# Float32r halves for the output projection and the memory projections of block two, with weight slots that step around the gates

## The reference

```python
merged = (jax.nn.sigmoid(gate_a) * (y_a @ w_branch_a[l])
          + jax.nn.sigmoid(gate_b) * (y_b @ w_branch_b[l]))
x = x + merged @ w_out[l]
x = x + memory_attention(rms_norm_2(x, norm_mem[l]), rms_norm_2(mem, mem_tok_norm[l]), mem_wq[l],
                         mem_wkv[l], mem_q_norm[l], mem_k_norm[l], mem_wo[l])
...
def memory_attention(h, mem_n, wq, wkv, q_norm, k_norm, wo):
    q = rms_norm_2((h @ wq).reshape(bsz, seqlen, MEM_HEADS, MEM_HEAD_DIM_2), q_norm)
    k, v = split_cols(mem_n @ wkv, (MEM_DIM, MEM_DIM))
    k = rms_norm_2(k.reshape(bsz, n_mem, MEM_HEADS, MEM_HEAD_DIM_2), k_norm)
    ...
```

## Time and profile before

| | us |
|---|---|
| Median of three runs | 3002.8 |
| The three runs | 2996.65, 3004.51, 3002.8 |
| The profiled execution | 2996.5 |
| Its span in the trace | 2994.6 |
| TensorE busy | 2785.1 (93%) |
| VectorE busy | 1494.3 (50%) |
| ScalarE busy | 1028.2 (34%) |
| GpSimd busy | 129.5 (4%) |
| Mean granted clock of TensorE | 0.978 |

### The profile page before, as it was taken

One profiled execution on the slowest core, in us unless ns is written; L12 is line 12 of the kernel. 1 busy time (PEld: TensorE's weight loads), 2 busy tenths in 40 slices (PEclk: granted clock), 3 DMA queues, 4 the chain that ended last, 5 costly groups with the idle time before them and its releaser, 6 DMA issues.

```text
span 2994.6 us, 34749 instructions
## 1 busy us (share of the span) xinstructions
PE 2785.1 (93%) x14923; PEld 2081.0 (69%) x14923; DVE 1494.3 (50%) x1648; ACT 1028.2 (34%) x1226; POOL 129.5 (4%) x109
## 2 busy tenths in 40 slices
PE   8999989999998999989879999998799899999998
PEld 6786576887887667864546468845474578888887
DVE  3555425455455126442573354425643347566587
ACT  3433233434434034320310144313201245454465
POOL 0002000000021000000011000000110000000000
PEclk9999999999999999999989999999899899999999
DMA  6554234556543335544331435543314157566696
GB/s 252 204 181 141 71 127 163 188 183 206 197 155 113 132 122 183 197 146 135 113 96 58 156 133 191 172 163 103 112 45 142 42 205 247 189 223 213 212 318 239
DMA packets 226565, 484.03 MB, mean 162 GB/s; under 512 B 11534, under 2 KB 44942, under 8 KB 225966
## 3 DMA queue, kind: packets, MB, share of 16 engines
q1 hardware_dynamic: 226032, 478.16, 47.0%
q10 hardware_dynamic: 380, 3.66, 0.4%
HBM read 477.07 MB, written 2.95 MB: 160 GB/s over the span
## 4 chain that ended last, share of the span: by engine, by line
PE 83%; DVE 10%; ACT 2%; DMA 2%; issue 2%; SPq 0%; POOL 0%; ACTq 0%; DVEq 0%; POOLq 0%
PE psum L411 21%; PE psum L408 17%; PE psum L410 16%; PE psum L409 16%; PE psum L2126 2%; PE psum L529 1%; PE psum L2856 1%; PE psum L2212 1%; DVE weight_ring_low_halves L403 1%; PE psum L909 1%; DVE stage_area_halves L520 1%; DMA weight_ring<-in_ffn_w_gate 1%; PE psum L621 1%; DVE small L961 1%; ACT weight_high_halves L397 1%
## 5 line engine op out<-in xcount | busy, mean ns | idle before, releaser
L403 DVE TENSOR_TENSOR weight_ring_low_halves<-weight_ring,weight_high_halves 128x2048 fp32r<-128x2048 f32 (+2 forms) x296 | 654.1, 2223 | 608.9 <-ACT weight_high_halves L397 608.9
L408 PE MATMUL psum<-weight_high_halves,stage_area_halves 128*128 128x512 f32 (+2 forms) x2266 | 872.2, 385 | 50.4 <-DVE stage_area_halves L520 34.4
L410 PE MATMUL psum<-weight_high_halves,stage_area_halves 128*128 128x512 f32 (+2 forms) x2266 | 863.3, 381 | 0.0
L409 PE MATMUL psum<-weight_ring_low_halves,stage_area_halves 128*128 128x512 f32 (+3 forms) x2060 | 785.2, 381 | 0.0
L397 ACT ACTIVATE weight_high_halves<-weight_ring 128x2048 fp32r<-128x2048 f32 (+2 forms) x296 | 549.1, 1866 | 532.6 <-PE psum L410 315.6
L411 PE MATMUL psum<-weight_ring,stage_area 128*128 128x512 f32 (+2 forms) x1600 | 666.3, 577 | 9.2 <-issue 6.6
L411 PEld LDWEIGHTS psum<-weight_ring,stage_area 128*128 128x128 f32 x1600 | 301.5, 191 | 357.5 <-issue 352.4
L408 PEld LDWEIGHTS psum<-weight_high_halves,stage_area_halves 128*128 128x128 f32 x2266 | 428.6, 189 | 139.7 <-DVE stage_area_halves L520 26.2
L410 PEld LDWEIGHTS psum<-weight_high_halves,stage_area_halves 128*128 128x128 f32 x2266 | 428.5, 189 | 85.9
L409 PEld LDWEIGHTS psum<-weight_ring_low_halves,stage_area_halves 128*128 128x128 f32 x2060 | 389.6, 189 | 74.9
L510 ACT ACTIVATE stage_area<-psum 128x512 f32<-128x512 f32 (+3 forms) x138 | 76.5, 562 | 683.3 <-PE psum L411 363.4
(11 more groups left out here) (287 smaller groups left out, 2169.2 us busy)
## 6 DMA issues: line engine op xcount, KB each, us to landing
weight_ring<-in_ffn_w_gate SPq DMA_DIRECT2D x44, 1024.0 KB, 5.2
weight_ring<-in_ffn_w_up SPq DMA_DIRECT2D x44, 1024.0 KB, 5.1
weight_ring<-in_ffn_w_down SPq DMA_DIRECT2D x44, 1024.0 KB, 5.0
weight_ring<-in_w_in SPq DMA_DIRECT2D x36, 1024.0 KB, 5.0
weight_ring<-in_moe_wd SPq DMA_DIRECT2D x30, 1024.0 KB, 5.0
weight_ring<-in_moe_wg SPq DMA_DIRECT2D x23, 1024.0 KB, 5.8
weight_ring<-in_moe_wu SPq DMA_DIRECT2D x23, 1024.0 KB, 6.6
weight_ring<-in_mem_w_kv SPq DMA_DIRECT2D x16, 1024.0 KB, 5.2
```

The lines of the kernel that those rows point to most:

```text
L403: v.raw.tensor_tensor(self.low_half(name), self.in_slot(name), self.high_half(name), ALU.subtract).then_inc(*v.mark("low_halves", ("halves ...
L408: pe.raw.matmul(out, a[1], w[0], start=start, stop=False)
L409: pe.raw.matmul(out, a[0], w[1], start=False, stop=False)
L410: return pe.raw.matmul(out, a[0], w[0], start=False, stop=stop)
```

## The change

The output projection and the memory's keys, queries and values of both layers are planned as split pieces and multiplied in halves. The turned rows that they read (`mergedT`, `memT` and the rows of `memx`) become pairs of halves, each with a second place in the stage area. The memory's own output projection stays plain.

Before the output projection's pieces, `skip_to_high_slot(2)` puts empty places into the list of split pieces, so that the first two pieces of the output projection take the high slots 2 and 3, and only the third and fourth the slots 0 and 1 under the gates; ScalarE waits for `groups_done` before it writes these. A split now waits for the last real piece in its high slot. Each layer has ten split pieces: four of the output projection, two each of keys, queries and values. The calls of `split_scalar` and `split_vector` for them are written into the two engines' programs between the existing steps.

```diff
--- before.py
+++ after.py
@@ -295,6 +295,10 @@
         if split:
             self.split_pieces.append(name)
 
+    def skip_to_high_slot(self, slot):
+        while len(self.split_pieces) % HIGH_SLOTS != slot:
+            self.split_pieces.append(None)
+
     def load_param(self, name, dst, src, after=(), topic=None):
 
         self.stream.append(("param", name, dst, src, after, topic or "loaded_" + "_".join(map(str, name))))
@@ -392,8 +396,9 @@
             i = self.split_pieces.index(name)
             act.wait_ge(*act.at(("loaded", name)))
 
-            if i >= HIGH_SLOTS:
-                act.wait_ge(*act.at(("used", self.split_pieces[i - HIGH_SLOTS])))
+            before = [p for p in self.split_pieces[i % HIGH_SLOTS:i:HIGH_SLOTS] if p is not None]
+            if before:
+                act.wait_ge(*act.at(("used", before[-1])))
             act.raw.activation(self.high_half(name), self.in_slot(name), ACT.Copy).then_inc(*act.mark("high_halves", ("high", name)))
 
     def split_vector(self, v, names):
@@ -1630,10 +1635,11 @@
 
         self.gate = [net.branch_gates[:, j * MT * D:(j + 1) * MT * D].rearrange("p (m n) -> p m n", m=MT) for j in range(2)]
         self.merged = net.part(E + 4096, MT, D)
-        self.mergedT = net.part(2048, KT, S)
+        self.mergedT = (net.halves_part(2048, KT, S), net.halves_part(0, KT, S))
 
         self.mem_tok = net.part(E, MT, D)
-        self.memT = net.part(E + 2048, KT, S)
+        self.memT = (net.halves_part(E + 2048, KT, S), net.halves_part(11264, KT, S))
+        self.xT_memx = (net.halves_part(0, KT, S), net.halves_part(2048, KT, S))
         self.q_tok = net.part(17408, MT, 512)
...
@@ -1686,15 +1692,16 @@
                     w = ins[f"w_branch_{'ab'[j]}_2"][l]
...
-            st["out"] = net.plan_proj(f"out{l}", ins["w_out_2"][l], blocks(D), KT)
+            net.skip_to_high_slot(2)
+            st["out"] = net.plan_proj(f"out{l}", ins["w_out_2"][l], blocks(D), KT, split=True)
             net.load_param(("mem_tok", l), self.mem_tok, ins["mem_2"].rearrange("b (m p) n -> p (b m) n", p=P),
                            [(("mergedT", l), m, kg) for m in range(MT) for kg in (0, 4)] + [("groups_done", l)])
             for j, name in enumerate(("mem_q_norm_2", "mem_k_norm_2")):
                 net.load_param(("mem_gain", l, j), self.mem_gain[:, j, :], row_broadcast(ins[name][l], P),
                                [("groups_done", l)], topic="loaded_mem_gain")
-            st["mk"] = net.plan_proj(f"mems{l}_k", ins["mem_wkv_2"][l][:, 0:512], blocks(512), KT)
-            st["mq"] = net.plan_proj(f"mems{l}_q", ins["mem_wq_2"][l], blocks(512), KT)
-            st["mv"] = net.plan_proj(f"mems{l}_v", ins["mem_wkv_2"][l][:, 512:D], blocks(512), KT)
+            st["mk"] = net.plan_proj(f"mems{l}_k", ins["mem_wkv_2"][l][:, 0:512], blocks(512), KT, split=True)
+            st["mq"] = net.plan_proj(f"mems{l}_q", ins["mem_wq_2"][l], blocks(512), KT, split=True)
+            st["mv"] = net.plan_proj(f"mems{l}_v", ins["mem_wkv_2"][l][:, 512:D], blocks(512), KT, split=True)
             st["mo"] = net.plan_proj(f"mems{l}_o", ins["mem_wo_2"][l], blocks(D), 4)
...
             self.merge_tensor(pe, l)
             net.turn_tensor(pe, self.merged_turn(l))
             turned = [[(("mergedT", l), m, kg) for kg in (0, 4)] for m in range(MT)]
-            net.proj_tensor(pe, st["out"], lambda k, m: self.mergedT[:, k, m * P:(m + 1) * P], self.out_bank, turned)
+            net.proj_tensor(pe, st["out"], lambda k, m: pick(self.mergedT, k, m), self.out_bank, turned)
             net.turn_tensor(pe, self.norm_turn(("memt", l), self.mem_tok, self.memT))
-            memT = lambda k, m: self.memT[:, k, m * P:(m + 1) * P]
+            memT = lambda k, m: pick(self.memT, k, m)
             net.proj_tensor(pe, st["mk"], memT, rot, self.turn_need(("memt", l)))
-            net.turn_tensor(pe, self.norm_turn(("memx", l), net.ax, net.xT))
-            net.proj_tensor(pe, st["mq"], xT, rot, self.turn_need(("memx", l)))
+            net.turn_tensor(pe, self.norm_turn(("memx", l), net.ax, self.xT_memx))
+            net.proj_tensor(pe, st["mq"], lambda k, m: pick(self.xT_memx, k, m), rot, self.turn_need(("memx", l)))
             net.turn_tensor(pe, self.small_turn(("mem_k", l), net.v_tok, net.kT))
             net.proj_tensor(pe, st["mv"], memT, rot)
...
@@ -2565,12 +2572,19 @@
             self.chunks_scalar(act, l)
             self.gate_scalar(act, l, 1, 1)
             net.turn_copy(act, self.ya_turn(l))
+            pieces = st["out"]["pieces"] + st["mk"]["pieces"] + st["mq"]["pieces"] + st["mv"]["pieces"]
+            net.split_scalar(act, pieces[:2])
             net.turn_copy(act, self.merged_turn(l))
+            act.wait_ge(*act.at(("groups_done", l)))
+            net.split_scalar(act, pieces[2:4])
             self.rms_scalar(act, ("memt", l), self.mem_tok, net.v_tok, lambda m: [("loaded", ("mem_tok", l))])
             net.turn_copy(act, self.norm_turn(("memt", l), self.mem_tok, self.memT))
+            net.split_scalar(act, pieces[4:6])
             self.rms_scalar(act, ("memx", l), net.x, net.ax, lambda m: [("x", n + 1, m)])
+            net.split_scalar(act, pieces[6:8])
             net.proj_copy(act, st["mk"], rot, self.mem_take(0))
-            net.turn_copy(act, self.norm_turn(("memx", l), net.ax, net.xT))
+            net.turn_copy(act, self.norm_turn(("memx", l), net.ax, self.xT_memx))
+            net.split_scalar(act, pieces[8:])
             net.proj_copy(act, st["mq"], rot, self.q_take)
             net.turn_copy(act, self.small_turn(("mem_k", l), net.v_tok, net.kT))
             net.proj_copy(act, st["mv"], rot, self.mem_take(1))
@@ -2617,17 +2631,23 @@
             self.finish_vector(v, l)
             net.turn_copy(v, self.ya_turn(l))
             self.merge_vector(v, l)
+            pieces = st["out"]["pieces"] + st["mk"]["pieces"] + st["mq"]["pieces"] + st["mv"]["pieces"]
+            net.split_vector(v, pieces[:2])
             net.turn_copy(v, self.merged_turn(l))
+            net.split_vector(v, pieces[2:4])
             self.rms_vector(v, ("memt", l), self.mem_tok, self.mem_tok, 2)
             net.turn_copy(v, self.norm_turn(("memt", l), self.mem_tok, self.memT))
+            net.split_vector(v, pieces[4:6])
             self.add_vector(v, n, lambda m: [(st["out"]["tag"], "full", b, m) for b in range(2)])
...
             self.rms_vector(v, ("memx", l), net.x, net.ax, 1)
-            net.turn_copy(v, self.norm_turn(("memx", l), net.ax, net.xT))
+            net.turn_copy(v, self.norm_turn(("memx", l), net.ax, self.xT_memx))
+            net.split_vector(v, pieces[6:8])
             v.wait_ge(*v.at(*net.proj_names(st["mk"]), ("loaded", ("mem_gain", l, 1))))
             self.heads_vector(v, ("memk", l), x4(net.v_tok[:, :, 0:512]), self.sk_tok, [(0, 4, self.mem_gain[:, 1, :])],
                               done=("heads_normed", ("mem_k", l)))
             net.turn_copy(v, self.small_turn(("mem_k", l), net.v_tok, net.kT))
+            net.split_vector(v, pieces[8:])
```

## The result

The changed kernel has a median of 3023.27 us (3020.2 to 3026.23, three runs) beside 3002.8 (2996.65 to 3004.51): a ratio of 1.007, 95% interval 1.0046 to 1.0095. Five more runs of the same code gave 1.0063 (1.005 to 1.0077). Both intervals leave out 1: it is slower by some 0.65%, by the medians 20.5 us in the first comparison and 17.3 in the second, where 10.9 were forecast. The profiled execution took 3023.27 us (span 3021.4, mean granted clock 0.968) against 2996.5 (2994.6, 0.978).

A forecast was written before the change was run, and what follows sets the result against it. TensorE was taken as the bound. Cheaper products -27.2, added waits +32.1 and clock falls +6.0 gave +10.9 us: 3007.4 on the profiled execution, 3013.5 stated on the median; range 3001 to 3025.

The forecast's parts named there:

- rival C: Clock falls at three stops a layer and stays low longer, 2.5 us each: +19.9 us, 3022.7; chance 0.17.
- What bounds the kernel: In the changed stage, TensorE's own time: blocks back to back, so a matmul saved is time saved unless TensorE waits.
- Saving, 27.2 us: 80 products a layer, each 0.693 us in halves instead of 0.863: 13.6 us a layer, 27.2 in both.
- Waits, 16.05 us a layer: TensorE's added waits before output projection, keys, queries and values: 4.85, 4.85, 3.6 and 2.75 us; 32.1 in both layers.
- Chains with 2 us of cover: Residual add and norms of keys' and queries' heads end before TensorE needs them, each with about 2 us left.
- Rival D: VectorE's chain is 4 us longer, so 2 us of wait at two places a layer: 3021.5; chance 0.08.
- The clock, two falls a layer at 1.5 us, 6.0 in all: Half clock on TensorE after empty stops of about 4.9 and 4.8 us; bounds 0 and 18.6 us.
- step 3: Queries: VectorE splits behind four low copies, so 5.9 us from first transpose against 2.34: 3.6 us added.
- the stated sign: From the last merge, values' last product about 2.5 us later than before without the clock, 5.5 with it.
- Rival A: Waits as computed, but the clock stays up: -27.2 + 32.1 = +4.9 us, 3007.7; chance 0.23.
- Rival B: Splits at the four turns are hidden and the kernel is faster: -20.8 us, 2982; chance 0.10.

The follow-up runs named there:

- the filled kernel: Changed kernel plus dummy float32 products on TensorE ahead of output projection, keys and queries (5, 5 and 4): 3011.66 us, 1.0035 of the kernel before.
- the version with all four moved: Changed kernel with output projection's first splits within the merge, and keys', queries' and values' splits ahead of the turned rows' copies: 2982.09 us, 0.9928 of the kernel before.
- the values' move: Changed kernel with only VectorE's two splits of the values put ahead of its copy of the turned keys: 3017.16 us, 1.0048 of the kernel before.

## Why the prediction was right, and which term was off

The mechanism was right: dearer waits eat the cheaper products, and the clock comes on top. That the time lies in the stated range is in part luck. The single forecast, 3013.5 us, was 9.8 us short, and the 3023.27 measured are inside because the range was drawn up to rival C, 3025. Over 3011.8 was to count as slower, which had 0.54. In the stage, both layers, the sum -27.2 + 32.1 + 6.0 = +10.9 came out as -26.0 + 33.8 + 15.0 = +22.8: all three errors point the same way, and the clock's is 9.0 of 11.9 us.

- **What bounds the kernel**: right. What was cut from or added to TensorE's line in this stage appeared in the whole: in the table above the stage and the ratio (its distance from 1 times 3003 us) agree within 3.5 us in every row. (The prediction speaks of five blocks; the stage has four.)
- **Saving, 27.2 us**: measured 26.0. At full clock the blocks are 22.27, 11.18, 11.18 and 11.17 us, where the earlier trace rows have 27.47, 13.81, 13.80 and 13.73: 13.0 a layer. The pace of the earlier trace rows carried over to the new place, 11.18 / 16 = 0.699 us a product. The rows, not the estimate from the count of passes, were the better measure.
- **Waits, 16.05 us a layer**: measured 16.9. From the last merge to the first product 1663.02 - 1657.15 = 5.87 us (5.8 forecast); keys 6.96 (6.7), queries 6.40 (5.9), values 3.74 (3.6). Taking off what stood there before (0.99, 1.87, 2.34, 0.88), that is 4.88, 5.09, 4.06 and 2.86. The pattern was the one that the earlier trace rows had shown once. Each of the four was short, by 0.03 to 0.5 us, within the 0.5 allowed. VectorE's load grew by 1545.3 - 1494.3 = 51 us, with 45 and more forecast.
- **Chains with 2 us of cover**: held. The norm of x that the queries' turn needs ended at 1703.95, and the keys' block at 1708.52, 4.6 us later, and TensorE has no wait for the norm of either kind of heads; the slower block gave it more cover, as was said against rival C. Rival D is out.
- **The clock, two falls a layer at 1.5 us, 6.0 in all**: this is the term that was mis-sized. Measured 15.0: three falls a layer, in the first of 2.97, 2.12 and 2.54 us. Two errors, both downward. The stop at the queries was left out because it was computed as 3.6 us and no row lay between 2.7 and 4.3. It came out at 4.02 us, since step 3 was short, and a fall followed it in both layers; whether one would have followed a stop of 3.6 us no run shows. And 1.5 us was taken near the lower end of 1.4 to 3.1, from a row where the low stretch was 2.9 us long; here it lasted 4.6 to 6.1 us of work. Rival C had both, with 2.5 us each, and its +19.9 is nearer to the stage's 22.8 than the forecast's 10.9. The two medians' differences, 20.5 and 17.3 us, lie about it too: the waits were the forecast's, the clock was C's. The same term is what the stated sign missed: counted from the last merge, the values' last product was to come 5.5 us later than before, and the next transposes came 86.40 - 74.89 = 11.5 us later, with 7.6 of it the clock's.
- **Rival A** (clock stays up) is refuted as what happened, and the filled kernel shows what it would have given: 7.6 us in the stage, where A said 4.9. **Rival B**'s point, 13.6 us of added waits a layer below which the change wins, is borne out from both sides: 16.9 loses even with the clock held up (the filled kernel), 1.9 in the version with all four moved wins.
- The page "TensorE: Matmul & The Clock Gate" of the Trainium skill (section Why this matters for your kernels) has idle gaps between bursts put TensorE back to half rate. The trace agrees, at 1.2 GHz behind all six stops of 4.0 to 5.1 us. Rival C, beside which it stood, was given 0.17.

What isn't settled: why one of two like stops of 2 to 3 us is followed by a fall and the other isn't, and how large the values' move is in the whole time.

## What to carry to other kernels

When a change makes the bounding engine's work cheaper but gives another engine preparation to do, first look where that preparation stands in its in-order queue. Ahead of data that the bounding engine is already waiting for, it costs its full length (the first pair of splits, 4.49 us, made the first wait 4.30 us longer). A block earlier, in an idle place of that queue, it costs next to nothing: here +20 us or -21 us with the same instructions. Price a new stop of TensorE of 4 to 5 us twice, as the wait and as the 2 to 3 us that the low clock cost behind it here. And where a computed stop lies between a row that fell and one that didn't, carry both outcomes through the sum: here the stop left out had a fall of 2.5 us a layer.
